# Sample attention: value pages in groups of four on four column tiles, sums picked with matmuls on chip

## The chip, the cores and the metric

The kernel runs on one core of one Trainium2 chip. The metric is the device time of one execution in microseconds (us). A core has five engines that run their own instruction streams and meet at semaphores: TensorE (PE in the profile, its weight loads PEld), VectorE (DVE), ScalarE (ACT), GpSimd (POOL) and SyncE (SP), which here issues most of the loads from HBM. The granted clock of TensorE is one of two levels in these traces, 2.4 GHz (shown as 1.0) and 1.2 GHz (0.5).

## What is computed

One layer of a hybrid decoder for a prompt of 512 tokens and a group of 8 sample tokens with the same weights. A combined projection feeds four branches (a short gated conv, a gated delta rule in four chunks of 128 tokens, a conformer conv, a forgetting attention), then a merge with gates, a cross attention and a feed-forward with a conv. The change touches one part, the forgetting attention of the 8 samples over their paged past:

```python
kp, vp, lp = past                      # 8 samples x 2048 tokens, in pages of 128 tokens
kk = jnp.concatenate([kp, fk], axis=1)
vv = jnp.concatenate([vp, fv], axis=1)
s = jnp.einsum('bqhd,bkhd->bhqk', qi, k) * (d ** -0.5)
s = s + jnp.swapaxes(ci, 1, 2)[..., None] - ck
p = jax.nn.softmax(s, axis=-1)
o = jnp.einsum('bhqk,bkhd->bqhd', p, v)     # 8 heads of 64
```

A sample has 16 pages, so there are 128 value pages. A page is 128 tokens by 512 numbers (8 heads of 64) in fp32, 256 KB. For a page, TensorE multiplies the 8 columns of probabilities (one per head) with the 512 columns of values. Of the 8 x 512 sums the reference needs only the 64 columns of each head's own block.

## The kernel before

All engines walk the same list, `TIMELINE`, made by `timeline()` (from L192). It lines up `piece` entries (half a tile of a weight matmul: 24 or 12 matmuls with 260 columns for each of the two halves), the evacuations of their results, and `side` entries, the steps of everything else (`SIDE`, L161). `step()` puts one side step after each piece half. A wait `AFTER` or `BEFORE` in `SIDE` ties steps to pieces. When pieces reach a `BEFORE` mark, `through()` puts all the steps up to it in a row, with no pieces between them; these are called bare steps below.

The side steps around the change are those of the gated delta rule, `("gdn", n, c)`, n from -1 to 17 in chunks c = 1 to 3, then `("gp", n)`, n from 0 to 4. They depend on each other: for a step K, ACT or DVE first works on what PE made in step K-1, and then PE does its matmuls of step K, with a wait for that work. In odd steps from n = 3 on the work in between is one ACT copy of 128x512; in even steps from 4 to 12 it is three DVE operations in a row; in n = 1 and 2 it is more DVE work; in n = 0 it is a long mix of both. n = 17 has no matmuls.

The value pages run in the background of these steps. `V_FILLED` and `V_BARE` are both 2: ahead of every side step PE does two pages (`page(i)` in the PE block). Pages 0 to 31 lie in 16 steps that have pieces between them, pages 32 to 127 in bare steps. The sums of a sample's 16 pages build up in partitions 0 to 7 of the PSUM bank `s3`. After the 16th page ACT copies the 8 x 512 sums to `vrow` and stores them to DRAM (`vscr`), waiting for PE's `v_used`; PE waits for this copy (`v_rows`) before the next sample. After the last sample ACT loads the 64 needed columns of each row back (`v64`), PE transposes them (step `df 0`, ahead of which it waits for the loads), and DVE makes the output columns (step `df 1`).

SP loads the pages into `kring`, a ring of four buffers in SBUF. Three pages are loaded at the start (`vstart`), and at the entry of page i SP waits for page i-1 to be used (`v_used`) and then loads page i+3:

```python
elif e[0] == "v" and e[1] + 3 < N_PAGE:
    if e[1] >= 1:
        sp.wait_ge(v_used.sem, e[1])
    page("cache_fox_v", e[1] + 3)
```

Each load takes SP a read of the page number from a table (L670) and the issue of the DMA (L671). An fp32 matmul call shows in the trace as two passes, each with its own weight load, one right after the other.

Of the kernel before, what the change touches and what calls it, by code (L numbers as in the profile page):

```python
# [53 lines left out]
(I_ID, I_ONE, I_UP, I_NEGLOW, I_CAUSAL, I_LO, I_HI, I_PAGE, I_LVL) = range(9)  # L54
# [8 lines left out]
def constants():  # L63
# [8 lines left out]
    out[:, I_LO] = r < FD  # L72
    out[:, I_HI] = r >= FD
# [77 lines left out]
def last_piece(kind):  # L151
# [6 lines left out]
V_FILLED, V_BARE = 2, 2  # L158
# [18 lines left out]
        + [("PAGES",), ("df", 0), ("df", 1)] + [("BEFORE", "gateD")]  # L177
# [10 lines left out]
N_PAGE = PAGES * NB  # L188


def timeline():

    out, pos, step_n, tile, at_piece, bg = [], [0], [0], [0], [-1], {"tap": None, "k": None, "v": None}
    size = {"tap": N_TAP, "k": N_PAGE, "v": N_PAGE}

    def background(kind, n):
        for done in range(n):
            if bg[kind] is not None and bg[kind] < size[kind]:
                if kind == "v" and bg[kind] % PAGES == 0 and done > 0 and n < 10:
                    return  # L200
                out.append((kind, bg[kind]))
                bg[kind] += 1

    def step(done, filled=True):

        while pos[0] < len(SIDE):
# [4 lines left out]
            elif s[0] in ("TAPS", "REDUCES", "PAGES"):  # L211
                background({"TAPS": "tap", "REDUCES": "k", "PAGES": "v"}[s[0]], 10 ** 6)
# [8 lines left out]
            elif s[0] != "BEFORE":  # L221
                background("v", V_FILLED if filled else V_BARE)
# [15 lines left out]
    def through(mark):  # L238
# [3 lines left out]
        while pos[0] < at and any(s[0] not in ("AFTER", "BEFORE") for s in SIDE[pos[0]:at]):  # L242
            step(10 ** 6, False)
# [69 lines left out]
assert [e[1] for e in TIMELINE if e[0] == "v"] == list(range(N_PAGE))  # L313
# [4 lines left out]
def pe_works(s):  # L318
# [3 lines left out]
                "ds": 3, "df": 1, "ex": 5, "xm": 2, "x": XU + 2, "xd": 3, "ef": 6, "y": 5,  # L322
# [23 lines left out]
def dve_works(s):  # L346
# [7 lines left out]
    if kind == "df":  # L354
        return n == 1
# [48 lines left out]
def build(nc, a, out):  # L404
    ctx = ExitStack()
    with ctx:
# [13 lines left out]
        cst = sb("cst", [P, N_CST * P + NB])  # L420
# [69 lines left out]

        def col(n):
# [7 lines left out]
        vscr = nc.dram_tensor("v_scratch", (NB * FH * (512 + FD),), F32, kind="Internal").ap()  # L499
# [23 lines left out]
        vs_out, v64_in = [sem(f"vs_out{n}") for n in range(2)], sem("v64_in")  # L523
# [43 lines left out]
        vrow, v64 = cb[:, :, 3:515], v(g3, 2, FD)  # L567
# [65 lines left out]
        def _(sp):  # L633
# [45 lines left out]
            for e in TIMELINE:  # L679
# [83 lines left out]
        def _(pe):  # L763
# [102 lines left out]
            def side(K, s):  # L866
# [124 lines left out]
                elif kind == "ds" and n == 0:  # L991
                    tr(s0[0:64, 0:P], mx64[:, :, :].rearrange("p a b -> p (a b)"))
                    f = qk32[:, :, :].rearrange("p a b -> p (a b)")
                    mm(s1[:, 0:32], cs(I_LO), f)
                    last = mm(s1[:, 32:64], cs(I_HI), f)
# [58 lines left out]
            def page(i):  # L1054

                if i == 0:
                    pe.wait_ge(dve_s.sem, upto(dve_works, ITEMS.index(("ds", 3)) + 1))
                elif i % PAGES == 0:
                    pe.wait_ge(v_rows.sem, i // PAGES)
                pe.wait_ge(page_in[i % 4], 16 * (N_PAGE // 4 + i // 4 + 1))  # L1060
                v_used.by(mm(s3[0:FH, :], sc[:, i, :], kring[:, i % 4, :], i % PAGES == 0, i % PAGES == PAGES - 1))

            for e in TIMELINE:
# [6 lines left out]
                elif e[0] == "v":  # L1070
                    page(e[1])
# [3 lines left out]
        def _(act):  # L1075
# [313 lines left out]
            for e in TIMELINE:  # L1389
# [542 lines left out]
```

## Time and profile before

| | us |
|---|---|
| median of 3 timed runs | 1887.08 (1886.43 to 1889.21) |
| span of the profiled execution, first to last instruction | 1882.9 |
| PE busy in it | 1620.8 |
| entries with pages between pieces (pages 0 to 31) | 747 to 832 |
| bare steps (pages 32 to 127, steps `gdn` and `gp`) | 832 to 1017 |
| start of the next weight matmuls (piece 76) | 1022.65 |

The median lies 4.2 us above the profiled span; that is what lies around the span, and it is added to every time worked out from it. In the timelines a row is a run of instructions: its start, its length, the engine, the line, what it writes and reads, the count, and in brackets the engine's idle time before it and what ended it. `sd` is the PSUM tensor whose bank 3 is `s3`; `pb` holds the sums of the pieces; `128*8 128x512` is a matmul with 128 rows and 8 columns of weights that streams 512 columns. Only value pages have this form.

### The profile page before, as it was taken

Reading aid. Unit: us, or ns where it says so; the run is one execution under the profiler, and the core shown is the slowest. Engines: PE = TensorE matmul, PEld = TensorE weight load, DVE = VectorE, ACT = ScalarE, POOL = GpSimd, SP = SyncE. Lnnn points to the kernel's source line nnn. Section 1 sums busy time; section 2 is a strip of 40 time slices with the busy share of each in tenths; the row PEclk is TensorE's granted clock in tenths of the full one; section 3 lists DMA queues with packets and bytes.
Section 4 is the critical chain, followed back from the end, with each engine's and each line's share of the span. In section 5 each row is a group of like instructions: output and inputs, shape, how many; then the busy total and the mean of one; then the engine's idle time right before and its main releaser. Section 6 shows DMA issues by size and latency. Waiting matters only on the chain. (4 is left out here: it accounts for less than half of the span.)

```text
span 1882.9 us, 28434 instructions
## 1 busy us (share of the span) xinstructions
PE 1620.8 (86%) x11148; PEld 1424.8 (76%) x11148; DVE 850.8 (45%) x1313; ACT 560.8 (30%) x903; POOL 635.0 (34%) x354
## 2 busy tenths in 40 slices
PE   4999899876687678998896899898677999999996
PEld 3999677666666677664443899898577899999996
DVE  4003777777986755313312122245322666663001
ACT  3334232235101322211115233345213333333222
POOL 1337444334466662100000344320402344444341
PEclk8999999888778798999998999999758899999998
DMA  6225322232346442444453522323312222332231
GB/s 196 74 85 175 96 91 96 79 101 90 94 123 187 128 130 76 137 135 135 124 147 97 182 91 90 124 68 101 112 56 68 68 90 92 99 100 75 94 100 46
DMA packets 154389, 200.02 MB, mean 106 GB/s; under 512 B 10180, under 2 KB 112125, under 8 KB 153848
## 3 DMA queue, kind: packets, MB, share of 16 engines
q1 hardware_dynamic: 137253, 169.46, 29.0%
q10 hardware_dynamic: 16011, 24.02, 3.8%
q0 software_dynamic: 992, 4.72, 0.8%
q8 instruction: 88, 1.44, 0.3%
q14 instruction: 45, 0.37, 0.1%
HBM read 187.92 MB, written 10.94 MB: 106 GB/s over the span
## 5 line engine op out<-in xcount | busy, mean ns | idle before, releaser
L726 POOL TENSOR_TENSOR wl<-raw,wh 128x1024 fp32r<-128x1024 f32 (+2 forms) x196 | 427.3, 2180 | 1098.9 <-ACT wh L1082 1097.3
L765 PE MATMUL pb<-xh,wh 128*128 128x260 f32 x2176 | 645.1, 296 | 37.2 <-DVE xl L1455 22.4
L765 PE MATMUL pb<-xl,wh 128*128 128x260 f32 x2176 | 628.7, 289 | 0.0
L765 PE MATMUL pb<-xh,wl 128*128 128x260 f32 x2176 | 627.0, 288 | 0.0
L765 PEld LDWEIGHTS pb<-xh,wh 128*128 128x128 f32 x2176 | 424.5, 195 | 55.1 <-issue 43.4
L765 PE MATMUL sd<-ar 128*128 128x128 f32 (+7 forms) x1584 | 359.9, 370 | 77.8 <-DVE ar L1455 26.0
L765 PEld LDWEIGHTS pb<-xl,wh 128*128 128x128 f32 x2176 | 425.7, 196 | 0.8
L765 PEld LDWEIGHTS pb<-xh,wl 128*128 128x128 f32 x2176 | 424.6, 195 | 0.0
L1082 ACT ACTIVATE wh<-raw 128x1024 fp32r<-128x1024 f32 (+2 forms) x208 | 201.6, 969 | 567.8 <-PE pb L765 541.0
L765 PEld LDWEIGHTS sd<-ar 128*128 128x128 f32 (+4 forms) x1584 | 208.0, 195 | 196.7 <-issue 136.7
L737 POOL TENSOR_TENSOR ar<-ar 128x512 f32<-128x512 f32 x128 | 179.6, 1403 | 93.6 <-DMA ar<-in_cache_fox_k 63.2
L765 PE MATMUL pb<-oh,wh 128*128 128x260 f32 (+1 forms) x384 | 119.6, 311 | 13.8 <-POOL wl L726 4.2
L769 PE MATMUL sd<-cst,ar 128*128 128x128 f32 (+6 forms) x360 | 65.4, 303 | 62.8 <-DVE ar L1455 26.3
L1593 DVE SCALAR_TENSOR_TENSOR ar<-xT,cols,ar 128x512 f32<-128x512 f32 x120 | 116.8, 1014 | 1.6
L765 PE MATMUL pb<-ol,wh 128*128 128x260 f32 (+1 forms) x384 | 114.2, 297 | 0.0
L765 PE MATMUL pb<-oh,wl 128*128 128x260 f32 (+1 forms) x384 | 114.1, 297 | 0.0
L765 PE MATMUL sd<-ar,cst 128*128 128x260 f32 (+7 forms) x216 | 64.7, 433 | 50.3 <-DVE ar L1663 19.3
L1600 DVE TENSOR_REDUCE ar<-ar 128x8 f32<-128x512 f32 x128 | 84.8, 679 | 49.3 <-POOL ar L737 48.8
L765 PE MATMUL pb<-hh,wh 128*128 128x260 f32 x352 | 101.2, 288 | 2.6 <-DVE hl L1455 2.6
L769 PEld LDWEIGHTS sd<-cst,ar 128*128 128x128 f32 (+6 forms) x360 | 43.7, 147 | 73.9 <-issue 51.4
L765 PE MATMUL pb<-hh,wl 128*128 128x260 f32 x352 | 99.5, 283 | 0.0
L765 PE MATMUL pb<-hl,wh 128*128 128x260 f32 x352 | 99.4, 282 | 0.0
(163 smaller groups left out, 1671.7 us busy)
## 6 DMA issues: line engine op xcount, KB each, us to landing
raw<-in_w_in SPq DMA_DIRECT2D x40, 1024.0 KB, 5.5
ar<-in_cache_fox_k SPq DMA_DIRECT2D x128, 256.0 KB, 2.8
ar<-in_cache_fox_v SPq DMA_DIRECT2D x128, 256.0 KB, 2.9
raw<-in_w_ffn_in SPq DMA_DIRECT2D x22, 1024.0 KB, 5.1
raw<-in_w_branch SPq DMA_DIRECT2D x16, 512.0 KB, 3.6
raw<-in_w_ffn_out SPq DMA_DIRECT2D x8, 1024.0 KB, 5.2
ar<-in_cache_mem_k ACTq DMA_DIRECT2D x1, 4096.0 KB, 20.1
raw<-in_w_out SPq DMA_DIRECT2D x4, 1024.0 KB, 5.3
```

The costliest lines, as they stand in the source:

```text
L726: pool.tensor_tensor(wl[:, p % 2, 0:kt, :], raw[:, u % 2, 0:kt, half * P:(half + 1) * P], wh[:, p % 2, 0:kt, :].bitcast(F32), SUB).then_in ...
L737: own(pool.tensor_tensor(kring[:, i % 4, :], kring[:, i % 4, :], qb[:, :], MUL), prod_done)
L765: return pe.matmul(o, l, r, start=start, stop=stop, skip_group_check=True)
L769: return pe.transpose(o, i, ident[0:n, 0:n])
L1082: own(act.activation(o, i, f, **kw), st)
L1593: dve_c.by(dve.scalar_tensor_tensor(out=oC[:, c, 0:SEQ], in0=g[:, j - 1:j - 1 + SEQ], scalar=w[:, j - 1:j], in1=oC[:, c, 0:SEQ], op0=MUL, ...
L1600: page_free.by(dve.tensor_reduce(sc[:, i, :], kring[:, i % 4, :].rearrange("p (h d) -> p h d", h=FH), AX, ADD))
```

## The change

Four pages go in one group. The weights of a group are the probabilities of its four pages side by side, 32 columns; page j of the group is streamed against them into partitions 32j to 32j+31 of `s3`, a column tile of its own. So every tile also gets the products of its page with the other three pages' probabilities, which are not used. After the 4 groups of a sample ACT copies all 128 x 512 sums, PE picks the right rows with four matmuls against a constant with 8 columns (into 32 columns of `s3`), and DVE copies the 8 numbers per partition that belong to the sample into `vnum`. The way over DRAM, the transpose and step `df 0` of before go; what was `df 1` is now `df 0`.

In the list, `values()` is called ahead of every side step and does by turns: the matmuls of a group (`v`), and in the next step the loads of the next group (`vload`) and, after a sample's last group, the picking (`vsel`). SP's loads of group g+1 wait until group g is used, since a group takes all four buffers of `kring`. PE waits for all four pages of a group ahead of its first matmul. The first group of a sample waits for the DVE copies of the sample before (`v_num`). Some constants are packed more closely; two matmuls of step `ds 0` read them as broadcast columns.

```diff
-V_FILLED, V_BARE = 2, 2
+V_GROUP = 4
...
+N_VG, V_PER = N_PAGE // V_GROUP, PAGES // V_GROUP
...
+    def values():
+
+        n = bg["v"]
+        if n is None or n >= 2 * N_VG:
+            return
+        g = n // 2
+        if n % 2 == 0:
+            out.append(("v", g))
+        else:
+            if g + 1 < N_VG:
+                out.append(("vload", g + 1))
+            if (g + 1) % V_PER == 0:
+                out.append(("vsel", g // V_PER))
+        bg["v"] += 1
...
-                background("v", V_FILLED if filled else V_BARE)
+                values()
                 out.append(("side", step_n[0], s))
...
                 elif e[0] == "vstart":
 
                     sp.wait_ge(pe_s.sem, upto(pe_works, ITEMS.index(("dc", 1)) + 1))
-                    for i in range(3):
+                    for i in range(V_GROUP):
                         page("cache_fox_v", i)
-                elif e[0] == "v" and e[1] + 3 < N_PAGE:
-                    if e[1] >= 1:
-                        sp.wait_ge(v_used.sem, e[1])
-                    page("cache_fox_v", e[1] + 3)
+                elif e[0] == "vload":
+
+                    sp.wait_ge(v_used.sem, e[1])
+                    for i in range(V_GROUP):
+                        page("cache_fox_v", V_GROUP * e[1] + i)
...
-                elif kind == "df" and n == 0:
-                    pe.wait_ge(v64_in, 32)
-                    last = tr(s3[:, 0:64], v64[0:NB * FH, :, :].rearrange("p a b -> p (a b)"))
...
-            def page(i):
-
-                if i == 0:
+            def pages(g):
+
+                if g == 0:
                     pe.wait_ge(dve_s.sem, upto(dve_works, ITEMS.index(("ds", 3)) + 1))
-                elif i % PAGES == 0:
-                    pe.wait_ge(v_rows.sem, i // PAGES)
-                pe.wait_ge(page_in[i % 4], 16 * (N_PAGE // 4 + i // 4 + 1))
-                v_used.by(mm(s3[0:FH, :], sc[:, i, :], kring[:, i % 4, :], i % PAGES == 0, i % PAGES == PAGES - 1))
+                elif g % V_PER == 0:
+                    pe.wait_ge(v_num.sem, g // V_PER)
+                for j in range(V_GROUP):
+                    pe.wait_ge(page_in[j], 16 * (N_PAGE // 4 + g + 1))
+                lhs = sc[:, V_GROUP * g:V_GROUP * (g + 1), :].rearrange("p i h -> p (i h)")
+                for j in range(V_GROUP):
+                    last = mm(s3[32 * j:32 * j + 32, :], lhs, kring[:, j, :], g % V_PER == 0, g % V_PER == V_PER - 1)
+                v_used.by(last)
+
+            def picked(b):
+
+                pe.wait_ge(v_rows.sem, b + 1)
+                for c in range(KB):
+                    last = mm(s3[:, c * FH:(c + 1) * FH], vrow[:, b % 2, c * P:(c + 1) * P], pick)
+                v_picked.by(last)
...
-                elif e[0] == "v" and e[1] % PAGES == PAGES - 1:
-                    b = e[1] // PAGES
+                elif e[0] == "v" and e[1] % V_PER == V_PER - 1:
+                    b = e[1] // V_PER
                     act.wait_ge(v_used.sem, e[1] + 1)
                     if b >= 2:
-                        act.wait_ge(vs_out[b % 2], 16 * (b // 2))
-                    fn(vrow[0:FH, b % 2, :], s3[0:FH, :], ACT.Copy, v_rows)
-                    at = b * FH * (512 + FD)
-                    store(vscr[at:at + FH * 512].rearrange("(h n) -> h n", h=FH), vrow[0:FH, b % 2, :], vs_out[b % 2])
-                    if b == NB - 1:
-
-                        for j in range(2):
-                            act.wait_ge(vs_out[j], 16 * NB // 2)
-                        for j in range(2):
-                            act.dma_start(v64[0:NB * FH, j, :], vscr.rearrange("(r n) -> r n", n=512 + FD)[:, 0:FD]).then_inc(v64_in, 16)
+                        act.wait_ge(v_picked.sem, b - 1)
+                    fn(vrow[:, b % 2, :], s3, ACT.Copy, v_rows)
...
+                elif e[0] == "vsel":
+                    b = e[1]
+                    dve.wait_ge(v_picked.sem, b + 1)
+                    for j in range(2):
+                        r = slice(FD * j, FD * j + FD)
+                        cp(vnum[r, :, b], s3[r, 0:KB * (FH + 2)].rearrange("p (c x) -> p c x", x=FH + 2)[:, :, j], v_num if j else dve_c)
```

## Rows read from the trace of the kernel before

**Rows 1.** The page: span and TensorE, with busy time and share
```profile
span 1882.9 us, 28434 instructions
PE 1620.8 (86%) x11148; PEld 1424.8 (76%) x11148; DVE 850.8 (45%) x1313; ACT 560.8 (30%) x903; POOL 635.0 (34%) x354
```
**Rows 2.** Busy time of each engine by stretch, with granted clock and DMA share
```profile
core 0: us, PE busy (x) PEld busy (x) DVE busy (x) ACT busy (x) POOL busy (x), PEclk, DMA share, GB/s
747.00:832.00 85.00, 85.00 (x521) 58.21 (x519) 23.36 (x43) 16.82 (x30) 13.84 (x8) 1.00 0.44 133
832.00:989.00 157.00, 138.59 (x641) 68.08 (x640) 41.71 (x86) 23.96 (x49) 0.00 (x0) 0.98 0.47 138
989.00:1023.00 34.00, 19.96 (x45) 5.49 (x44) 3.23 (x5) 19.34 (x22) 1.00 (x1) 0.89 0.36 100
917.00:931.00 14.00, 8.89 (x29) 3.80 (x29) 5.96 (x16) 4.51 (x12) 0.00 (x0) 0.76 0.31 95
860.00:890.00 30.00, 27.08 (x130) 13.52 (x128) 7.54 (x12) 2.98 (x5) 0.00 (x0) 1.00 0.47 134
```
**Rows 3.** TensorE timeline, bare steps: two starts of a step pair, and a long wait
```profile
866.35 6.74 PE L765 MATMUL sd<-ar 128*128 128x128 f32 x32 [0.26 <-DVE ar L1455]
873.40 6.74 PE L765 MATMUL sd<-ar 128*128 128x128 f32 x32 [0.31 <-DVE ar L1455]
924.14 6.09 PE L765 MATMUL sd<-ar 128*128 128x128 f32 x14 [5.11 <-ACT ar L1289]
```
**Rows 4.** VectorE and ScalarE in the same steps
```profile
871.37 0.69 DVE L1703 TENSOR_TENSOR ar<-ar,sd 128x512 f32<-128x512 f32 x1 [5.16 <-PE sd L765]
872.58 0.68 DVE L1455 TENSOR_TENSOR ar<-ar,sd 128x512 f32<-128x512 f32 x1
874.62 0.60 ACT L1291 ACTIVATE ar<-sd 128x512 f32<-128x512 f32 x1 [6.45 <-PE sd L765]
```
**Rows 5.** Weight loads and passes of pages, bare steps at either clock
```profile
901.17 0.09 PEld L765 LDWEIGHTS sd<-ar 128*8 128x8 f32 x1 [0.34 <-issue]
902.12 2.08 PEld L765 LDWEIGHTS sd<-ar 128*128 128x128 f32 x18 [0.86 <-issue]
926.96 0.14 PEld L765 LDWEIGHTS sd<-ar 128*8 128x8 f32 x1 [0.72 <-issue]
927.81 0.14 PEld L765 LDWEIGHTS sd<-ar 128*8 128x8 f32 x1 [0.72 <-issue]
```
**Rows 6.** TensorE by group: pages in bare steps; small matmuls with fresh weights
```profile
L765 PE MATMUL sd<-ar 128*8 128x512 f32 x192 | 93.5, 612 | 1.8 <-DMA ar<-in_cache_fox_v 1.7
L765 PE MATMUL sd<-ar 128*128 128x2 f32 x192 | 41.2, 352 | 9.7 <-issue 9.7
```
**Rows 7.** A page's second pass (x2 holds the next), and issues of page loads
```profile
900.74 1.02 PE L765 MATMUL sd<-ar 128*8 128x512 f32 x2
899.18 0.34 SPq L671 DMA_DIRECT2D ar<-in_cache_fox_v  x1
900.28 0.34 SPq L671 DMA_DIRECT2D ar<-in_cache_fox_v  x1
902.09 0.34 SPq L671 DMA_DIRECT2D ar<-in_cache_fox_v  x1
733.07 4.03 SPq L671 DMA_DIRECT2D ar<-in_cache_fox_v  x4
DMA to landing us min/median/max: 2.5/2.8/4.7
DMA to landing us min/median/max: 3.0/3.5/4.0
```
**Rows 8.** End of the pages: waits for pages, way over DRAM, next piece
```profile
1014.93 1.02 PE L765 MATMUL sd<-ar 128*8 128x512 f32 x2 [0.88 <-DMA ar<-in_cache_fox_v]
1022.38 0.33 PE L769 MATMUL sd<-cst,ar 64*128 64x64 f32 x1 [5.01 <-DMA ar<-v_scratch]
1022.65 0.58 PE L765 MATMUL pb<-xh,wh 128*128 128x260 f32 x1
```

More of the change, by code:

```diff
@@ L51 @@
 C_GATE = C_FF + FH
-(I_ID, I_ONE, I_UP, I_NEGLOW, I_CAUSAL, I_LO, I_HI, I_PAGE, I_LVL) = range(9)
+(I_ID, I_ONE, I_UP, I_NEGLOW, I_CAUSAL, I_SEL, I_PAGE, I_LVL) = range(8)
+S_LO, S_HI, S_PAGE, S_PICK = 0, 1, 2, 2 + NB
 N_CST = I_LVL + LEVELS
@@ L71, in constants @@
     out[:, I_CAUSAL] = np.where(c > r, np.float32(NEG), np.float32(0))
-    out[:, I_LO] = r < FD
-    out[:, I_HI] = r >= FD
+    out[:, I_SEL, S_LO:S_LO + 1] = r < FD
+    out[:, I_SEL, S_HI:S_HI + 1] = r >= FD
+    out[:, I_SEL, S_PAGE:S_PAGE + NB] = r // PAGES == np.arange(NB)[None]
+    out[:, I_SEL, S_PICK:S_PICK + FH] = (r // 32 == r % 32 // FH) & (r % FH == np.arange(FH)[None])
     out[:, I_PAGE] = (r // PAGES == c // PAGES) & (r < c)
@@ L188, with step @@
 N_PAGE = PAGES * NB
+N_VG, V_PER = N_PAGE // V_GROUP, PAGES // V_GROUP
 def timeline():
     out, pos, step_n, tile, at_piece, bg = [], [0], [0], [0], [-1], {"tap": None, "k": None, "v": None}
-    size = {"tap": N_TAP, "k": N_PAGE, "v": N_PAGE}
+    size = {"tap": N_TAP, "k": N_PAGE}
     def background(kind, n):
-        for done in range(n):
+        for _ in range(n):
             if bg[kind] is not None and bg[kind] < size[kind]:
-                if kind == "v" and bg[kind] % PAGES == 0 and done > 0 and n < 10:
-                    return
                 out.append((kind, bg[kind]))
                 bg[kind] += 1
-    def step(done, filled=True):
+    def values():
[11 more added lines that the diff above has]
+        bg["v"] += 1
+    def step(done):
         while pos[0] < len(SIDE):
@@ L210, in step @@
                     return
-            elif s[0] in ("TAPS", "REDUCES", "PAGES"):
-                background({"TAPS": "tap", "REDUCES": "k", "PAGES": "v"}[s[0]], 10 ** 6)
+            elif s[0] == "PAGES":
+                while bg["v"] < 2 * N_VG:
+                    values()
+            elif s[0] in ("TAPS", "REDUCES"):
+                background({"TAPS": "tap", "REDUCES": "k"}[s[0]], 10 ** 6)
                 if s[0] == "REDUCES":
@@ L242, in through @@
         while pos[0] < at and any(s[0] not in ("AFTER", "BEFORE") for s in SIDE[pos[0]:at]):
-            step(10 ** 6, False)
+            step(10 ** 6)
     def norm(i, squares=True):
@@ L312 @@
 assert [e[1] for e in TIMELINE if e[0] == "k"] == list(range(N_PAGE))
-assert [e[1] for e in TIMELINE if e[0] == "v"] == list(range(N_PAGE))
+assert [e[1] for e in TIMELINE if e[0] == "v"] == list(range(N_VG))
 assert TIMELINE.index(("tap", N_TAP - 1)) < TIMELINE.index(("piece", first_piece("brA") + 6, 0))
@@ L489, in cs, with picks @@
             return cst[:, n * P:(n + 1) * P]
+        def picks(n, k):
+            return cst[:, I_SEL * P + n:I_SEL * P + n + k]
         def col(n):
@@ L522, in build @@
         wsm_hi, wsm_lo, v_rows = stage("gate_weights_hi"), stage("gate_weights_lo"), stage("v_rows")
-        vs_out, v64_in = [sem(f"vs_out{n}") for n in range(2)], sem("v64_in")
+        v_picked, v_num = stage("v_picked"), stage("v_numerators")
         dve_v = stage("dve_other")
@@ L566, in build @@
         qk32, m1, pn, rd64 = v(g3 + 144, 4, NB), v(g3 + 176, 1), v(g3 + 192, NB, FH), v(g3 + 256, NB, FH)
-        vrow, v64 = cb[:, :, 3:515], v(g3, 2, FD)
+        vrow, vnum = cb[:, :, 3:515], v(g3, KB, NB)
+        pick = picks(S_PICK, FH)
         mx64, mb, rs64, dg64 = v(g3 + 320, NB, FH), v(g3 + 384, NB, FH), v(g3 + 448, NB, FH), v(SQ, 64)
@@ L993, in side @@
                     f = qk32[:, :, :].rearrange("p a b -> p (a b)")
-                    mm(s1[:, 0:32], cs(I_LO), f)
-                    last = mm(s1[:, 32:64], cs(I_HI), f)
+                    mm(s1[:, 0:32], picks(S_LO, 1).to_broadcast([P, P]), f)
+                    last = mm(s1[:, 32:64], picks(S_HI, 1).to_broadcast([P, P]), f)
                 elif kind == "ds" and n == 1:
@@ L1070, in _ @@
                 elif e[0] == "v":
-                    page(e[1])
+                    pages(e[1])
+                elif e[0] == "vsel":
+                    picked(e[1])
         @block.scalar
@@ L1771, in side @@
                         red(tot, lf[:, :, :].rearrange("p t h -> p h t"), ADD)
-                        tt(totm[:, :, :], spread(tot, NB, 1), spread(cst[:, N_CST * P:N_CST * P + NB], FH, 2), MUL, dve_s)
+                        tt(totm[:, :, :], spread(tot, NB, 1), spread(picks(S_PAGE, NB), FH, 2), MUL, dve_s)
                     elif n == 1:
@@ L1923 @@
         a[name] = nc.dram_tensor(f"in_{name}", x.shape, mybir.dt.from_np(x.dtype), kind="ExternalInput").ap()
-    r = np.arange(P)[:, None]
-    arrays["in_cst"] = np.concatenate([constants(), (r // PAGES == np.arange(NB)[None]).astype(np.float32)], axis=1)
+    arrays["in_cst"] = constants()
     a["cst"] = nc.dram_tensor("in_cst", arrays["in_cst"].shape, F32, kind="ExternalInput").ap()
```

13 lines of the change are left out of this document (6 added, 7 removed).

## Prediction

> **What bounds the kernel now.** I read the profile's page first, then the stretches, then single steps. TensorE is busy for 1620.8 of 1882.9 us, no other engine for more than 45% [rows 1]. The pages lie in three stretches [rows 2]. From 747 to 832 (pages 0 to 31, pieces between the steps) PE is busy all 85 us: it is the bound, and whatever is taken from it is gained until something else is late. From 832 to 989 (bare steps) it is busy for 138.6 of 157 us, but here pages are filler: ahead of each side step ACT or DVE works on what PE just made, and PE does two pages meanwhile. A pair of steps (one odd, one even, four pages) takes 7.05 us, from 866.35 to 873.40 [rows 3], and PE then still waits 0.31 us for DVE. From 989 on the norm steps hold PE back (20 of 34 us busy).
>
> A page is two passes 0.43 us apart (0.09 + 0.34 between two weight loads), 0.86 us [rows 5]. The 192 passes of the bare steps take 93.5 us as a union [rows 6], and they waited 1.7 us in all for their loads. That is the row to keep in mind: with three pages loaded ahead the loads are hidden.
>
> **The matmuls of a group.** There are still 128 calls and 256 passes of 512 columns; only where they overlap is time won. No pair of neighbours in this trace goes to different column tiles, so I bound it. From the first pass of a group to its last: 7 x 0.43 = 3.01 us if nothing overlaps, 0.43 us if all four tiles run together. Between the two lies what the order of the passes suggests: the two passes of a page use the same tile and follow each other, PE starts its matmuls in order, so only a page's second pass and the next page's first can overlap. Then the last starts after 4 x 0.43 = 1.72 us. I take that one. Below nothing it cannot go, as a second pass needs the first one's tile.
>
> By the Trainium skill (TensorE: Matmul & The Clock Gate, Part 3) matmuls start and end strictly in order, and three column tiles gave 2.38 times the speed; no row here shows either. By the first my middle value would hold.
>
> Entering and leaving the narrow form costs more than a plain change of matmul: the next wide weight load comes 0.95 us after the last narrow one (0.09 + 0.86) instead of 0.43 + 0.43 [rows 5], so about 0.09 us each way. That halves with the runs of pages, some 6 us in all of PE time, included below.
>
> **The loads, which nothing hides any more.** Before, page i+3 is asked for when page i-1 is done. Now a group owns all four buffers, SP waits for its last matmul, and PE waits for the fourth load. So load and use take turns. From the last pass of a group: the second pass of a page starts at 900.74, SP's issue that waited for it comes at 902.09, so 1.35 us [rows 7]; three more issues at 1.11 us each (899.18 to 900.28), 3.32 us; landing 2.5 to 4.7 us, median 2.8, and 3.0 to 4.0 where four were issued in a row, I take 3.0; waking PE 0.05 us. Sum 7.7 us. With 1.72 us for the group itself, a pair of steps can't be shorter than 9.4 us.
>
> What it has to hide behind are the two steps' own matmuls and one ACT copy: a run of 8 and one of 16 passes at 0.11 us, and about 1.0 us from matmuls to matmuls over the copy of 0.60 us [rows 4]; 0.5 us to leave the narrow form. That makes 4.4 us in pairs where DVE's three operations lie under the group, 5.8 us in the others (2.4 instead of 1.0 us: 0.36 to start, 871.37 to 873.26 for the three, and the wake). Both are below 7.7. So bare pairs go from 7.05 to 9.4 us, though PE has less to do.
>
> **The picking.** Four calls are 8 passes with 8 columns and fresh 128-column weights; 192 such passes with 2 columns took 41.2 us, 0.215 each [rows 6]: 1.7 us per sample, 13.7 in all (lower bound 0.11 each, 7 us; the upper one would be 0.43 each). In bare steps they lie in the wait for loads and cost nothing; if that cover were gone, they'd be 10 us. DVE has the picked sums to copy ahead of its own work of that step, and is blocked until PE has picked. Where that step needs DVE (n = 6 and 14 of chunk 1, 0 and 8 of chunk 3) the chain is longer by the picks and two copies of about 0.2 us. ACT's copy grows from 8 to 128 partitions at the same 512 columns, so about 0.6 us as its copies of 128x512 [rows 4]; without the store behind it, it is no worse than before.
>
> **Sum, 747 to 832.** Per pair of steps, one run of pages goes (1.29 + 0.43 + 2 x 0.09 = 1.9 us) and the other gets 0.43 longer: -1.5 us, eight pairs -11.8. Added: two pickings 3.4; DVE's work after them (three operations for n = 6, one for n = 14) with PE idle, 3.0 + 1.3; waits for DVE or ACT that the second run of pages covered, about 0.85 us in each of two steps with a short piece half (2.4 against 1.55 us) and an estimated 1.4 in n = 0, 3.1 together; pairs stretched to 9.4 us or to that and the 0.5 us of a weight load in SP's queue, 3. Total +2 us. So here the gain is spent again.
>
> **Sum, from 832.** 23 intervals from group 8 to group 31 at 9.4 us make 216.2; two of them (chunk 3, n = 0 and n = 8, DVE behind the picks) take 1.5 more each. After the start of group 31: 1.72 + 0.68 to ACT's start + 0.6 copy + 1.7 picks, 4.8 with the wakes, to the next piece. Together 224.0. Before it is 1022.65 - 832.1 = 190.5 [rows 8], in which the way over DRAM (the 5.01 us wait) is counted: that gain is inside. +33.5 us.
>
> **The clock.** In 14 or so of the 24 groups PE will have idled over 3 us ahead of the group. After the 5.11 us wait before 924.14 [rows 3] the granted clock of 917 to 931 is 0.76 on average, partly 1.2 GHz, while 860 to 890, with PE busy for 27.1 of 30 us, has 1.00 [rows 2]. At the lower clock passes are 0.85 us apart (926.96 to 927.81) [rows 5], which makes a group up to 1.7 us longer, and this is on the path, since the loads wait for its end. I take 1.3 us each, +18 us; bounds 0 and 24 x 1.7 = 41.
>
> **Total.** 1882.9 + 2 + 33.5 + 18 = 1936.4, and with the 4.2 us around the span 1940.6 us. After the pages PE's work is unchanged, so the delay goes through to the end. Own range of this case 1918 to 1965. The narrower constants and the broadcast weights of step ds 0 cost nothing: the same number of matmuls.
>
> **Rivals.**
> 1. *Column tiles don't overlap* (the change doesn't do what it says). 3.01 instead of 1.72 us per group on the path: 24 x 1.29 = 31, 6 more in the first stretch, and 12 more at the low clock: 1990 us, from 1965 to 2010. For it: both weight loads and streams were only ever seen one after the other. Chance 0.30.
> 2. *All four run together.* 0.43 instead of 1.72: 31 and some 6 us less, and less lost to the clock: 1897 us. Against it: two passes of a page share a tile. The Trainium skill (TensorEngine Tiling (Array Packing), Theoretical Speedup) gives up to four times for four column tiles; by that rule this case would hold. Chance 0.12.
> 3. *The loads stay hidden, and the kernel is faster.* The place is the wait for the fourth page; it decides at 4.4 to 5.8 us from a group's last pass to the next group. Were four loads there in that time (one issue for all or issues far under 1.11 us), bare pairs would be about 7.1 us or less with the group at 1.72, DVE's chain and the picks included, and the 5 us at the end are won: 52 us below the forecast without clock loss of 18, so near 1870. Against it: SP's issues alone are 3.3 us, the landing 2.5 at the least [rows 7], and where PE had nothing but pages to do it waited for them even at three ahead, 0.88 us at 1014.93 [rows 8]. Chance 0.06.
> 4. The rest, 0.48 for the forecast and 0.04 for something near no change (overlap of all, and a shorter landing).
>
> **How the numbers follow.** A measurement of this kernel can tell about 0.2%, 3.8 us. Faster by more only in rival 3, 0.06; same 0.04; slower 0.90. The range from 1903 to 2005 holds the forecast case, rival 1 but its end, and the upper part of rival 2; it is that wide because the overlap of the passes is not to be seen in this trace.
>
> **What the profile after would show.** Passes of pages in pairs at the same start, a group 1.7 us from first to last start: right; 3.0 or 0.4: rival 1 or 2. PE waiting for the loads of the value pages with 2 to 3.5 us ahead of nearly each bare group, 50 us and more in total against 1.7 before: right; under 10 us: rival 3. Step pairs of 9.4 us. A granted clock well below 0.98 in the bare steps. Pages to piece 76 in 224 us and more. The prediction is wrong at its root if the loads of a group are found landing before PE is through with the steps between.

## The result, and the profile after

The changed kernel takes 1913.86 us (1911.87 to 1916.82), the kernel before 1888.14 us beside it: 1.0134 times as long, 95% interval 1.0113 to 1.0155. Forecast were 1940.6 us, from 1903 to 2005, and 0.90 for slower. The side and the range hold; the size does not: 25.7 us instead of 53.5. The profiled execution has a span of 1913.9 us. All medians are of executions in one and the same state; one execution of the kernel without loads, 1926.09 us at a granted clock of 0.79 where the others had 0.90, is left out of its median.

The stretches of after, as rows 2 have them for before (first row 747 to 832, then the bare steps, then up to and behind the last groups; busy us of each engine, granted clock, DMA share, GB/s):

```profile
747.00:832.00 85.00, 72.59 (x574) 62.66 (x573) 25.55 (x47) 18.02 (x32) 14.42 (x8) 0.96 0.46 141
832.00:989.00 157.00, 99.90 (x557) 70.69 (x555) 39.42 (x87) 19.30 (x41) 0.00 (x0) 0.75 0.39 115
989.00:1023.00 34.00, 20.02 (x108) 14.26 (x108) 4.68 (x11) 8.15 (x11) 0.00 (x0) 0.75 0.40 119
1023.00:1050.00 27.00, 15.20 (x53) 8.47 (x50) 4.56 (x10) 14.82 (x17) 2.36 (x1) 0.50 0.27 78
```

In the bare steps TensorE is busy for 99.9 of 157 us where it was 138.6 [rows 2]: its work shrank, and the time did not. The granted clock is 0.75 there, a mixture of 1.2 and 2.4 GHz, where it was 0.98.

A group at 2.4 GHz. First what is busy in the 0.07 us from 871.83 on (the row of a stretch, TensorE and its weight loads first; in brackets how many instructions):

```profile
871.83:871.90 0.07, 0.06 (x4) 0.07 (x8) 0.00 (x0) 0.00 (x0) 0.00 (x0) 1.00 0.00 0
```

Then the timeline: a group alone (863.51), and two others with the loads between them (x16 counts neighbours of another shape in). The first two run at 2.4 GHz, the one at 879.98 at 1.2 GHz. SPq is the queue in which SyncE issues DMAs:

```profile
863.51 1.06 PE L787 MATMUL sd<-ar 128*32 128x512 f32 x8 [2.50 <-DMA ar<-in_cache_fox_v]
...
871.81 0.19 PEld L787 LDWEIGHTS sd<-ar 128*32 128x32 f32 x8 [3.56 <-issue]
871.84 2.82 PE L787 MATMUL sd<-ar 128*32 128x512 f32 x16 [3.40 <-DMA ar<-in_cache_fox_v]
...
873.68 3.62 SPq L692 DMA_DIRECT2D ar<-in_cache_fox_v  x4
874.75 0.60 ACT L1323 ACTIVATE ar<-sd 128x512 f32<-128x512 f32 x1 [8.40 <-PE sd L787]
...
879.98 1.94 PE L787 MATMUL sd<-ar 128*32 128x512 f32 x8 [0.80 <-DMA ar<-in_cache_fox_v]
```

Four of the eight passes are under way within 0.07 us, and all eight weight loads of the group are done within 0.19 us. A group takes 1.06 us at 2.4 GHz, the last pass included; that pass lasts 0.59 us, so 0.47 us lie between the first start and the last. At 1.2 GHz it is 1.94 us, 0.87 from start to start. The loads behind the group are as forecast: SP's first issue 1.36 us after the last start (872.32), four issues over 3.62 us, and the next group at 879.98, 7.7 us after the last pass of the one before.

What TensorE waited for, from 832 to 1050, the largest in after, and two of them in before (us in all, times, longest):

```profile
PE sd L787 <- DMA ar<-in_cache_fox_v: 42.3, 17, 4.7
PE sd L787 <- DVE ar L1479: 16.1, 9, 2.8
PE sd L787 <- DVE ar L1485: 8.2, 2, 5.0
PE sd L787 <- ACT ar L1323: 4.3, 5, 1.4
```
```profile
PE sd L765 <- DVE ar L1455: 4.0, 11, 1.0
PE sd L765 <- DMA ar<-in_cache_fox_v: 1.7, 3, 0.9
```

Timeline of the last group and of piece 76:

```profile
1042.81 1.94 PE L787 MATMUL sd<-ar 128*32 128x512 f32 x8 [2.82 <-DMA ar<-in_cache_fox_v]
1047.23 0.57 PE L787 MATMUL pb<-xh,wh 128*128 128x260 f32 x1
```

Group 8 starts at 827.53, group 31 at 1042.81, piece 76 at 1047.23. From group 8 to piece 76 these are 219.7 us, where the same steps took 190.5 (832.1 to 1022.65): 29.2 more. From group 0 to group 8 it is 79.2 us (748.31 to 827.53) against 84.6: 5.4 less. Piece 76 is 24.6 us late. Behind it TensorE does the same work in both, but this profile of after has 866.6 us from there to the end and the one of before 860.3; the profiles of the experiments have 862.1 to 867.9. These 6 us are not explained, and the single profile of before may just be a quick one: the medians are only 25.7 us apart, and the accounts below go by piece 76.

### The profile page after: what moved, and what is told of

Its sections match the earlier page's. It is cut to its first block and busy times, and to the rows that moved or that the text cites. A ratio compares the mean times of both kernels' runs of the same rounds, so it can differ in the third digit from the quotient of the medians.

```text
span 1913.9 us, 28626 instructions
## 1 busy us (share of the span) xinstructions
PE 1589.3 (83%) x11211; PEld 1453.5 (76%) x11211; DVE 854.6 (45%) x1329; ACT 560.8 (29%) x903; POOL 634.8 (33%) x354
## 5 line engine op out<-in xcount | busy, mean ns | idle before, releaser
L787 PE MATMUL sd<-ar 128*128 128x128 f32 (+7 forms) x1584 | 306.9, 421 | 143.5 <-DVE ar L1479 43.9
L787 PEld LDWEIGHTS sd<-ar 128*128 128x128 f32 (+4 forms) x1584 | 215.5, 217 | 199.6 <-issue 144.6
L791 PE MATMUL sd<-cst,ar 128*128 128x128 f32 (+7 forms) x359 | 69.2, 317 | 56.5 <-DVE ar L1479 25.9
L791 PEld LDWEIGHTS sd<-cst,ar 128*128 128x128 f32 (+7 forms) x359 | 46.9, 156 | 68.3 <-issue 47.1
```

The source lines that it names most:

```text
L787: return pe.matmul(o, l, r, start=start, stop=stop, skip_group_check=True)
L791: return pe.transpose(o, i, ident[0:n, 0:n])
```

## The experiments

Thirteen kernels ran. Theory: the four tiles do overlap, the loads of a group that nothing hides cost more than that wins, and the idle time costs clock on top. Rivals are named with each run. Ratios are to the kernel before on the same chip, with 95% intervals; differences are between medians, and across sets of runs they are good to some 4 us (the median of before was 1888.1 to 1892.2 in them).

**One tile.** All four pages go to partitions 0 to 31:

```diff
-last = mm(s3[32 * j:32 * j + 32, :], lhs, kring[:, j, :], g % V_PER == 0, g % V_PER == V_PER - 1)
+last = mm(s3[0:32, :], lhs, kring[:, j, :], g % V_PER == 0 and j == 0, g % V_PER == V_PER - 1 and j == 3)
```

> The changed kernel with all four pages of a group going to the same column tile (partitions 0 to 31), so that their sums mix; loads, picks and order as they are. In the changed kernel a group takes 0.47 us from its first pass to its last (871.84 to 872.32). Theory (the tiles overlap completely and the group is on the path, since the loads wait for its end): nothing overlaps any more, 7 x 0.43 = 3.01 us, 2.54 more for each of the 24 bare groups, 61 us, and up to 20 in the filled stretch, less what a busier TensorE gets back from the clock: 1913.9 + 55 to 80 = 1969 to 1994. Rival (the passes overlap for another reason than the tiles, or the waits for the loads take up the difference): within 6 us of 1914.

Measured: 2024.94 us, ratio 1.0724 (1.0685 to 1.0763), 111 us above the changed kernel. Timeline of a group at 2.4 GHz, and part of one at 1.2 GHz:

```profile
903.77 4.46 PE L787 MATMUL sd<-ar 128*32 128x512 f32 x14 [3.07 <-DMA ar<-in_cache_fox_v]
904.20 0.11 PEld L787 LDWEIGHTS sd<-ar 128*32 128x32 f32 x1 [0.32 <-issue]
904.63 0.11 PEld L787 LDWEIGHTS sd<-ar 128*32 128x32 f32 x1 [0.32 <-issue]
...
938.18 0.18 PEld L787 LDWEIGHTS sd<-ar 128*32 128x32 f32 x1 [0.68 <-issue]
939.03 0.18 PEld L787 LDWEIGHTS sd<-ar 128*32 128x32 f32 x1 [0.68 <-issue]
```

The weight loads come one per pass again, 0.43 us apart, seven times 0.43 in a group: 3.0 us. So the tiles are what makes the passes overlap. The time lies above both expectations because these long groups often run at 1.2 GHz (18 of the 24 bare ones at least in part), 0.85 us per pass and up to 5.95 from the first pass to the last, which I had not put in. What the tiles save is worth twice as much at the low clock: 5.1 us a group instead of 2.5.

**No loads.** SP loads no value pages from group 8 on:

```diff
-elif e[0] == "vload":
+elif e[0] == "vload" and e[1] < 8:
...
-pe.wait_ge(page_in[j], 16 * (N_PAGE // 4 + g + 1))
+pe.wait_ge(page_in[j], 16 * (N_PAGE // 4 + min(g, 7) + 1))
```

> The changed kernel without the loads of value pages from group 8 on; the matmuls use the pages that lie in the ring. Part of the work is left out. Theory (the exposed loads set the bare steps): a group then waits for the steps between alone, 5 to 6 us a pair instead of 9.4, so group 8 to piece 76 takes 125 to 150 us instead of 219.7, and the kernel 1820 to 1845. Rival (the narrow form, the picks and the low clock make the bare steps long): the pairs stay above 8 us and the kernel above 1885.

Measured: 1866.57 us, ratio 0.988 (0.9834 to 0.9926). 47 us less than the changed kernel, so the loads are the loss; but I had expected 69 to 94 less, and 125 to 150 us from group 8 to piece 76, where it takes 171.9. Timeline of a pair of steps, TensorE and VectorE:

```profile
860.39 1.13 PE L787 MATMUL sd<-ar 128*128 128x128 f32 x8 [1.13 <-DVE ar L1479]
862.25 3.05 PE L787 MATMUL sd<-ar 128*128 128x128 f32 x24 [0.74 <-ACT ar L1323]
866.43 1.13 PE L787 MATMUL sd<-ar 128*128 128x128 f32 x8 [1.13 <-DVE ar L1479]
...
858.35 0.69 DVE L1727 TENSOR_TENSOR ar<-ar,sd 128x512 f32<-128x512 f32 x1 [3.32 <-PE sd L787]
858.96 0.69 DVE L1728 TENSOR_TENSOR ar<-ar,cst 128x512 f32<-128x512 f32 x1
859.56 0.68 DVE L1479 TENSOR_TENSOR ar<-ar,sd 128x512 f32<-128x512 f32 x1
```

A pair without any wait for pages is 6.04 us (860.39 to 866.43): the chain of the steps itself, with its group in it. Against 7.05 [rows 3] that is 1.0 us a pair, by my estimate some 24 us for all, with the 5 us of the way over DRAM to come. It is no ceiling: from group 8 to piece 76 this run saves 18.6 us against before (171.9 and 190.5), with pairs of 7.7 between those of 6.0 and a clock of 0.84 from 832 to 989, and the best run below, at 0.92, saves 33.6 (156.9).

**Eight buffers.** The second four lie where the conformer output lay, which is dead by then; groups take the two rings by turns, with semaphores of their own:

```diff
-kring = v(DEC, 4, 512)
+kring, kring2 = v(DEC, 4, 512), v(OC, 4, 512)
...
-for i in range(V_GROUP):
-    page("cache_fox_v", i)
-elif e[0] == "vload":
+for i in range(2 * V_GROUP):
+    vpage(i // V_GROUP, i % V_GROUP)
+elif e[0] == "vload" and e[1] + 1 < N_VG:
...
-for i in range(V_GROUP):
-    page("cache_fox_v", V_GROUP * e[1] + i)
+for j in range(V_GROUP):
+    vpage(e[1] + 1, j)
```

> The changed kernel with eight page buffers instead of four (the second four where the conformer output lay), so that a group is loaded while the one before is used. Theory (the gain of the tiles is there and only the exposed loads hide it): TensorE waits for no loads, bare pairs take 5.3 to 6.3 us, group 8 to piece 76 takes 130 to 155 us, the kernel 1825 to 1850, clearly below the 1888 of the kernel before. Rival 1 (DVE's waits for the picks and the chain of copies take the place of the loads): pairs of 7 us and more, 1870 to 1890. Rival 2 (four issues of 1.11 us and the transfers themselves are the pace): pairs of 6.5 to 7.5 us, TensorE still waiting for loads, 1860 to 1880.

Measured: 1863.97 us, ratio 0.9869 (0.9831 to 0.9907). The expected side, but outside the expected 1825 to 1850, with 168.0 us from group 8 to piece 76 instead of 130 to 155. The time would fit rival 2, but TensorE waits for no loads; what is left is the chain of the steps, as without loads. What TensorE waits for from 832 to 1000 (the largest; the loads of pages are gone, and VectorE is first):

```profile
PE sd L796 <- DVE ar L1491: 20.9, 13, 2.8
PE sd L796 <- DVE ar L1497: 12.3, 3, 5.0
PE sd L796 <- ACT ar L1333: 7.1, 2, 4.0
```

**Eight buffers on one tile.** Both edits together.

> The kernel with eight buffers and all pages on one column tile, so that their sums mix. What four tiles are worth once the loads are hidden. Theory (2.5 us more per group, of which 1.2 lie in TensorE's wait for VectorE where the group stands ahead of an even step; the clock gives some of it back): 20 to 45 us more than with four tiles (1864): 1884 to 1909. Rival (the groups are filler beside the chain of steps, and the tiles give nothing; what eight buffers won is the hidden loads and the way over DRAM alone): 1860 to 1872.

Measured: 1929.15 us, ratio 1.0206 (1.0185 to 1.0227), 65 us more than with four tiles (64 by the ratios), above the expected 20 to 45. A group on one tile at 2.4 GHz, in the timeline:

```profile
863.04 3.62 PE L796 MATMUL sd<-ar 128*32 128x512 f32 x8
```

With the loads out of the way the tiles are worth 65 us, but against a schedule that is itself bad: all else of the change, on one tile and with eight buffers, costs 37 us against before. Of that the picks are 6 us by the later run without them in VectorE's way; that the rest is the grouping (four pages in every other step, 3.6 us in one place, where two in each step fitted the waits) is argued, not shown.

**Two pages on two tiles in every step.** `values()` gives two pages ahead of each step, on tiles 0 and 1, then 2 and 3; SP waits for the last pair and loads the one after next, with four buffers:

```diff
-for j in range(V_GROUP):
-    last = mm(s3[32 * j:32 * j + 32, :], lhs, kring[:, j, :], g % V_PER == 0, g % V_PER == V_PER - 1)
+for j in (2 * (p % 2), 2 * (p % 2) + 1):
+    last = mm(s3[32 * j:32 * j + 32, :], lhs, kring[:, j, :], p % 8 < 2, p % 8 > 5)
...
-sp.wait_ge(v_used.sem, e[1])
-for i in range(V_GROUP):
-    page("cache_fox_v", V_GROUP * e[1] + i)
+sp.wait_ge(v_used.sem, e[1])
+for i in range(V_PAIR):
+    page("cache_fox_v", V_PAIR * (e[1] + 1) + i)
```

> The changed kernel with two pages ahead of each side step on two of the four column tiles (0 and 1, then 2 and 3) instead of four in every other step, and the two pages after next loaded as soon as two are used, as before the change; four buffers. Theory (the loads of a group that wait for the whole group are the loss; the tiles are a gain): a load has two steps to land in, 1.35 + 2 x 1.11 + 3.0 = 6.6 us, about what the two steps take by themselves (6.0 us a pair in the runs without exposed loads, and 0.5 more for going into the narrow form twice), so pairs of 6.5 to 7.0 us, the kernel at 1868 to 1885. Rival (two tiles at a time give nothing over one, or the way of the picks costs what is won): pairs of 7 us and more, 1888 or above.

Measured: 1895.23 us, ratio 1.0028 (1.0007 to 1.0049): 19 us less than the changed kernel, but not below before, and in the range of the rival. But its first reason does not hold, that two tiles give nothing over one. Two pages in the timeline:

```profile
831.50 1.05 PE L789 MATMUL sd<-ar 128*32 128x512 f32 x4 [1.11 <-DMA ar<-in_cache_fox_v]
```

From the first start to the last it is 0.46 us (1.05 less the last pass, 0.59), as with four pages: two tiles overlap as well as four do. In TensorE's waits from 832 to 1020 of this run the pages still stand:

```profile
PE sd L789 <- DMA ar<-in_cache_fox_v: 23.4, 15, 3.0
```

My sum of 6.6 us left no margin over steps of 6.5, so the loads are exposed again wherever the steps are quick. In neither of the two ways tried were four buffers enough for pages that are used faster.

**Two queues.** From group 8 on GpSimd issues pages 2 and 3 of a group:

```diff
-for i in range(V_GROUP):
+for i in range(V_GROUP if e[1] < 8 else 2):
     page("cache_fox_v", V_GROUP * e[1] + i)
...
+elif e[0] == "vload" and e[1] >= 8:
+    pool.wait_ge(v_used.sem, e[1])
+    for j in range(2, V_GROUP):
+        i = V_GROUP * e[1] + j
+        n = pool.value_load(ptr_[0:1, i:i + 1], min_val=0, max_val=a["cache_fox_v"].shape[0] - 1)
+        pool.dma_start(kring[:, j, :], a["cache_fox_v"][bass.ds(n, 1)].rearrange("a p l h d -> (a p) (l h d)"))\
+            .then_inc(pool_in[j - 2], 16)
```

> The changed kernel with two of a group's four loads issued by GpSimd's queue instead of SyncE's, from group 8 on. Theory (the four issues of 1.11 us one after the other are 3.3 us of the 7.7 us from a group's end to the next): 1.35 + 1.11 + 3.0 = 5.5 us and 0.47 for the group make 6.0, as long as the chain of the steps itself, so bare pairs of 6.0 to 7.0, the kernel at 1868 to 1888. Rival (the transfers need that time whoever issues them, or GpSimd's issue is slow): intervals stay at 8 us and more, 1900 to 1915.

Measured: 1898.16 us, ratio 1.0052 (1.0026 to 1.0079): 16 us less than the changed kernel, between the two. Timeline, GpSimd's issues and the group behind them:

```profile
860.49 0.54 POOL L778 DMA_DIRECT2D ar<-in_cache_fox_v  x1 [5.99 <-issue]
...
861.63 0.55 POOL L778 DMA_DIRECT2D ar<-in_cache_fox_v  x1 [0.60 <-issue]
...
865.53 2.15 PE L795 MATMUL sd<-ar 128*32 128x512 f32 x16 [2.31 <-DMA ar<-in_cache_fox_v]
```

GpSimd's last issue comes at 861.63 instead of after four in a row, but the group starts 3.9 us later, and not 3.0. It waits for SP's second load: issued at 861.16, it lands at 865.44, after 4.3 us, and GpSimd's last one at 865.25. SP's four loads from 860 to 870, from issue to landing:

```profile
DMA to landing us min/median/max: 2.6/3.5/4.8
```

In all the groups from 9 on SP's second load takes 4.2 us (median), where in the changed kernel each but the first takes 2.9. From the first issue to the last landing of a group it is 5.4 us instead of 6.3, though the last issue comes some 1.7 us sooner: loads that are under way together take longer. 13 of the 23 bare pairs are 7.3 to 8.0 us, the others longer. So the issues in a row are only a part of the 7.7 us, and the rival is half right: the transfers take much of that time whoever issues them.

**No picks.** No picking matmuls and no copies of their sums; the next sample waits for `v_rows`:

```diff
-pe.wait_ge(v_num.sem, g // V_PER)
+pe.wait_ge(v_rows.sem, g // V_PER)
...
-elif e[0] == "vsel":
-    picked(e[1])
```

> The changed kernel without the picking: no picking matmuls, no copies of the picked numbers on VectorE, and the next sample waits for ScalarE's copy alone. Part of the work is left out. Theory (the picks lie in the wait for the loads but for some four places where VectorE's own work stands behind them): 4 to 12 us less, 1902 to 1910. Rival (VectorE held up by the picks is a main part of the loss): 20 us less and more, below 1894.

Measured: 1901.7 us, ratio 1.0059 (1.0038 to 1.0079): 12 us less, in the profiles 6.8 before group 8 (72.4 us instead of 79.2) and 6.6 behind it. Here is the place in the changed kernel, a single step with n = 6:

```profile
778.04 2.05 PE L787 MATMUL sd<-ar 128*128 128x128 f32 x16 [1.40 <-ACT ar L1323]
...
781.37 0.95 PE L787 MATMUL sd<-cst,ar 128*128 128x8 f32 x8
781.62 1.06 ACT L1114 ACTIVATE wh<-raw 128x1024 fp32r<-128x1024 f32 x1 [3.63 <-PE pb L787]
782.43 0.36 DVE L1488 COPY ar<-sd 64x4 f32<-64x4 f32 x2 [8.43 <-PE sd L787]
782.76 2.34 POOL L748 TENSOR_TENSOR wl<-raw,wh 128x1024 fp32r<-128x1024 f32 x1 [6.51 <-ACT wh L1114]
782.83 0.69 DVE L1727 TENSOR_TENSOR ar<-ar,sd 128x512 f32<-128x512 f32 x1
783.43 2.21 DVE L1728 TENSOR_TENSOR ar<-ar,cst 128x512 f32<-128x512 f32 x1
...
786.39 2.05 PE L787 MATMUL sd<-ar 128*128 128x128 f32 x8 [4.06 <-DVE ar L1479]
```

The picks are cheap, 0.95 us. But VectorE, idle for 8.43 us, could have begun its three operations with the end of the step before (780.1); it begins them only after the picks and their copies, at 782.83, and then the second meets a GpSimd operation and takes 2.21 us instead of 0.68 [rows 4]. The first meets it too and takes its usual 0.69 us. The difference between them is that the first reads PSUM (`sd`) and the second two tensors in SBUF: it ends at 785.64, 0.54 us behind GpSimd's (785.10). TensorE waits 4.06 us.

**Later copies.** VectorE copies the picked numbers behind its own work of the step:

```diff
-elif e[0] == "vsel":
+elif e[0] == "vnum":
...
+                if out[-2][0] == "vsel":
+                    out.append(("vnum", out[-2][1]))
```

> The changed kernel (four buffers) with VectorE copying the picked numbers behind its own work of that side step instead of ahead of it; nothing is left out. Theory (VectorE's wait for the picks is what leaving the picks out took away: 7 us at one place of the filled stretch and as much in the bare steps, of 12 us): 1902 to 1908. Rival (what costs is that the next group waits for the copies, so that their later place only moves the loss): 1911 to 1917.

Measured: 1905.86 us, ratio 1.0072 (1.0047 to 1.0097), 8 us less (12 by the ratios); group 0 to 8 takes 72.3 us, as without picks. From group 8 to piece 76 it is 217.6 us, only 2.1 less than in the changed kernel, where leaving the picks out took 6.6. With eight buffers and this edit:

> The kernel with eight page buffers, and VectorE copies the picked numbers behind its own work of that side step instead of ahead of it. Theory (with the loads hidden the chain of the side steps is the bound, and VectorE's wait for the picks is in it at eight places, 1.5 to 2.5 us each where its own work is long): 4 to 12 us less than with eight buffers alone (1864), 1852 to 1860. Rival (the picks cost nothing there either, or the next group's wait for the copies costs the same): within 3 us of 1864.

Measured: 1857.58 us, ratio 0.9819 (0.9767 to 0.9871), 6 us less than with eight buffers alone (9 by the ratios). The range is met, but not at the eight places that I named: in the profiles, from group 0 to 8 it is 70.3 us instead of 79.8, from group 8 to piece 76 it is 171.0 instead of 168.0, at a clock of 0.80 instead of 0.85 from 832 to 989. So the order on VectorE is the whole price of the picks in the filled stretch, mostly at n = 6; for the bare steps these runs show a third of it with four buffers and nothing with eight.

**Matmuls on constants in the waits.** Their results are read by nobody; all else is done. First, five calls ahead of each bare group:

```diff
+if g >= 9:
+    for j in range(5):
+        mm(pb[:, 0, 0, TH:512], ones, cst[:, 0:512 - TH])
```

> The changed kernel with five more fp32 matmuls of 252 columns on constants ahead of each group from 9 on, into PSUM columns that nothing reads; at 2.4 GHz they take some 2.2 us, and TensorE waits 3 us and more for the loads there. Theory (the idle time costs the clock, and the clock costs 0.4 us in the group and as much again in the side steps): the granted clock of 832 to 989 goes from 0.75 to 0.95 and more, the groups at 1.2 GHz (9.0 to 9.2 us apart) go to 8.2, 10 to 20 us less: 1894 to 1904. Rival (the clock costs nothing, since the loads set the pace): within 4 us of 1914, or more if the added matmuls get in the way.

Measured: 1917.45 us, ratio 1.0152 (1.0098 to 1.0205). The clock of 832 to 989 rose to 0.89 only, since the longest waits are elsewhere, and after those the five calls ran at 1.2 GHz, up to 3.6 us, with the pages already there. The added calls were in the way, and the run says nothing on the price of the clock. Then calls sized by the waits, three ahead of a group and six, two and four ahead of n = 0, 1 and 2:

> The changed kernel with matmuls on constants (252 columns, into PSUM that nothing reads; 0.38 us a call at 2.4 GHz) where TensorE waits in the bare steps: three calls ahead of each group, six ahead of step n = 0, two and four ahead of n = 1 and 2. Theory (the clock falls in the long waits, and costs 0.4 us in each group and as much in the steps): granted clock of 832 to 989 from 0.75 to 0.93 and more, piece 76 at 1025 to 1037 instead of 1047, the kernel 1893 to 1905. Rival (the loads set the pace at either clock): within 4 us of 1914.

Measured: 1913.07 us, ratio 1.0127 (1.0087 to 1.0167). The stretch 832 to 989 of this run:

```profile
832.00:989.00 157.00, 114.32 (x721) 84.45 (x719) 41.21 (x89) 19.90 (x42) 0.00 (x0) 0.93 0.40 119
```

The clock is back at 0.93, piece 76 comes 5 us sooner (4.4 counted from group 8), and the time is the same within its interval, as the rival has it. By the two intervals the gain is 10 us at most, so my 18 were too many. It is a gain net of what the calls cost: some groups follow them with no wait for pages (935.42, 972.30), so they may hold a group up, and this run can't tell the two apart. With hidden loads it is another matter. Calls of the same kind on the kernel with eight buffers and later copies, none ahead of the groups, two ahead of the even steps, and six, two and four ahead of n = 0, 1 and 2 as before:

> The kernel with eight buffers and the later copies, with the same matmuls on constants in the waits of its bare steps: two calls ahead of the even steps n = 4 to 12, where TensorE waits 1.7 us for VectorE, six, two and four ahead of n = 0, 1 and 2. Theory (with the loads hidden the steps' own matmuls are on the path, 24 passes per pair that take 0.11 or 0.22 us by the clock): granted clock of 832 to 989 from 0.85 to 0.95 and more, pairs of 7.7 us go to 6.1, 8 to 18 us less than without (1857.6): 1840 to 1850. Rival (the added matmuls delay what they wait beside by as much as the clock gives): 1855 and above.

Measured: 1841.65 us, ratio 0.9722 (0.9693 to 0.9751), 16 us less than without (18 by the ratios). Its stretch 832 to 900, and that of the kernel without these calls:

```profile
832.00:900.00 68.00, 59.73 (x412) 44.04 (x412) 27.77 (x63) 14.02 (x31) 0.00 (x0) 1.00 0.61 177
```
```profile
832.00:900.00 68.00, 49.53 (x316) 38.12 (x316) 22.11 (x48) 12.82 (x28) 0.00 (x0) 0.82 0.54 158
```

Without the calls pairs of 6.0 and of 7.7 us took turns; now all four from group 12 on are 6.0. More such calls in the last steps:

> The kernel with eight buffers, later copies and matmuls on constants in the waits, with six more such calls ahead of each of the steps gp 1 to 4, where TensorE waits some 4.2 us and its clock is at 1.2 GHz. Theory (two groups, two steps and the start of piece 76 run at 2.4 GHz then, 2 to 4 us): 1836 to 1842 where it was 1841.65 without them, 0.970 of the kernel before. Rival (the added matmuls are longer than the wait where the clock is still low, and nothing is won): 1842 to 1848.

Measured: 1841.68 us, ratio 0.9742 (0.9717 to 0.9767): nothing more. Group 31 came 2 us earlier than without them in the profile, below what the times can tell.

The best version is eight buffers with later copies and the calls on constants: 2.8% below before and 3.8% below the changed kernel (1841.65 against 1913.86). Without calls that compute nothing it is 1857.58.

## Why the prediction was right in its side and wrong in its size

*What bounds the kernel, the loads.* Right. I read from before that pages are filler in the bare steps and that taking all four buffers at once exposes the loads; 7.7 us from the last pass to the next group were forecast and 7.66 measured, and hiding the loads takes 50 us away (1863.97 against 1913.86). This term made the forecast's side right.

*The matmuls of a group.* The failed step. I took 1.72 us from first to last pass, since a page's two passes share a tile and TensorE starts in order. The first reason holds only for those two; the order does not keep the four tiles apart: four passes start together, and their four second passes follow 0.43 us later, 0.47 in all. That was the lower bound, 0.43, which I gave 0.12 as rival 2. It takes 1.25 us from each of 23 intervals, 28.8 us. That this is the whole miss (piece 76 is 24.6 us late, forecast 53.5) is partly luck: the clock (14 us) and the stretch from 747 to 832 (7) were forecast too dear as well, and pairs longer than I had them took some 21 us of that back. By the Trainium skill (TensorEngine Tiling (Array Packing), Theoretical Speedup), four column tiles give up to four times the speed. The runs bear it out: from the start of a group to its end 3.6 us on one tile (3.0 and the last pass of 0.59) and 1.06 on four, 3.4 times. Rival 2's own time, 1897, is still 17 us too low, by the next three points.

*The clock.* It fell well below 0.98 as forecast, to 0.75, but the price was wrong: 18 us forecast, 4.4 by the run that gives it back (net of the added calls) and 10 at most by its interval. With groups of 0.47 us there was only 0.4 us per group to lose (15 of the 24 ran at 1.2 GHz, 6 us), and where a wait for loads follows, slower steps run within that wait. A clock of 0.80 instead of 0.92 costs 16 us once the loads are hidden.

*The bare pairs.* From 871.84 to 879.98 a pair at 2.4 GHz takes 8.14 us (0.48 and 7.66), and hardly one takes less; 23 of them and 4.4 us at the end are 191.6, and 219.7 were measured. So 28.1 us lie above that floor where I had 21 (clock 18, two places 3). In order of size: pairs whose own chain is longer, as n = 0 and the `gp` steps with waits of up to 5.0 us for VectorE; 12.8 us if I take the intervals of the run without loads wherever they exceed 8.14. Then the picks, 6.6, and the clock, 4.4. Some 4 us are not assigned, and the parts may overlap. The forecast held only two pairs longer than the rest, by 1.5 us.

*The picks.* 8 passes take 0.95 us where I had 1.7, and the reason is a misread row. The 0.215 us per pass of [rows 6] come from passes that all ran at 1.2 GHz, as the first 64 of them show (stretch before 523.30); where the picks run at 1.2 GHz they take as long (after):

```profile
509.70:523.30 13.60, 13.56 (x64) 13.59 (x64) 7.65 (x8) 0.00 (x0) 8.41 (x8) 0.50 0.56 175
```
```profile
1045.50 1.88 PE L787 MATMUL sd<-cst,ar 128*128 128x8 f32 x8 [0.76 <-ACT ar L1114]
```

VectorE's wait was seen, but priced at 3.0 us in step n = 6. It was 6.4: the interval from group 3 to 4 is 17.0 us, and 10.6 with later copies. What I missed is what VectorE's work meets when it starts later, an operation of GpSimd, behind whose end one of its operations ends, after 2.21 us instead of 0.68. The two errors are opposite, so the sum for the picks in this stretch came out near, 7.7 us forecast and 6.8 measured.

*747 to 832.* Forecast +2, measured -5.4 from group 0 to 8. The overlap took more from TensorE than the half overlap in my sum (eight groups, 1.25 us each); the picks took 7 us back, as much as the sum had.

*Rivals.* No overlap is refuted by the weight loads in a row on one tile; its 1990 would have been too low, 2025. Hidden loads and a faster kernel, near 1870: wrong for this change, but eight buffers give that, 1864.

*Views forecast.* Groups 8.1 to 12 us apart, not 9.4 flat. TensorE's wait for pages 42.3 us up to 1050 where I wrote 50 and more. Piece 76 after 219.7 us where I wrote 224.

## What to carry to other kernels

Work that fills another chain's waits can only win what it sticks out by: here 7.05 against 6.04 us a pair in the bare steps, an estimated 24 us, and more only when the chain itself got quicker. A group that takes all buffers of a ring turns hidden loads into a wait of issue, landing and wake; double the ring with the group, and put an engine's new small task behind its chain work. What the clock costs depends on what follows: nothing that the times can tell before a wait for loads, 16 us where the chain itself was the bound. And look up the clock of a row before its durations go into a sum.

## What the runs showed of the hardware that was not expected

- The first passes of fp32 matmuls on four column tiles start within 0.07 us, the four second ones 0.43 us later (0.83 at 1.2 GHz), with all eight weight loads done in 0.19 us; on one tile each load waits for its pass, 0.32 us idle at 2.4 GHz and 0.68 at 1.2.
- Passes with 8 columns and a fresh 128-column weight load take 0.95 us for 8 at 2.4 GHz and 1.88 at 1.2 GHz; the two-column ones of [rows 6] ran at 1.2 GHz, 0.215 us each.
- A VectorE operation of 128x512 fp32 that reads only SBUF and began at least 0.2 us ahead of the end of a GpSimd operation (an elementwise one over two tensors) ended 0.54 to 0.56 us behind that end, in all fifteen profiles: it took 0.8 to 2.3 us instead of 0.68. One that reads PSUM took 0.67 to 0.69 us beside such operations.
- Halving the issues in a row (two queues) brought the shortest pairs from 8.1 us to 7.3, not to 6: a load issued by GpSimd took 3.5 us to land (median), and SyncE's second of a group 4.2 instead of 2.9.
